# Gate-matrix stores issued from GpSimd, exponentials and first dots one step later

## The reference

```python
def peer(x, w_q, sub_keys, u, v):            # x: 512 x 1024
    qb = (xb @ w_q).reshape(TOKEN_BLOCK, 8, 2, 128)
    s = jnp.einsum('thcd,hcnd->thcn', qb, sub_keys)
    s_top, i_top = lax.top_k(s, 16)           # 16 of 128 keys, for each half
    cand = s_top[:, :, 0, :, None] + s_top[:, :, 1, None, :]
    best, pos = lax.top_k(cand, 16)           # 16 of 256 pairs; expert = i0*128 + i1
    g = jax.nn.softmax(best, axis=-1)
    h = jax.nn.gelu(jnp.einsum('td,thkd->thk', xb, u[eidx]))
    return jnp.einsum('thk,thkd->td', g * h, v[eidx])
```

## Time and profile before

| | |
|---|---|
| Device time, three runs | 1592.0, 1596.01, 1598.8 us; median 1596.01 |
| Profiled execution, own time | 1596.0 us |
| Its span | 1594.2 us |
| TensorE busy | 1572.1 us, 99% of the span |
| VectorE busy | 1319.1 us, 83% |
| ScalarE busy | 647.3 us, 41% |
| GpSimd busy | 486.9 us, 31% |
| Granted clock of TensorE, mean | 0.996 |
| DMA | 452.24 MB, 284 GB/s on the mean |

### The profile page before, as it was taken

One profiled execution on the slowest core, in us unless ns is written; L12 is line 12 of the kernel. 1 busy time (PEld: TensorE's weight loads), 2 busy tenths in 40 slices (PEclk: granted clock), 3 DMA queues, 4 the chain that ended last, 5 costly groups with the idle time before them and its releaser, 6 DMA issues.

```text
span 1594.2 us, 24556 instructions
## 1 busy us (share of the span) xinstructions
PE 1572.1 (99%) x9566; PEld 1394.9 (88%) x9566; DVE 1319.1 (83%) x2408; ACT 647.3 (41%) x1012; POOL 486.9 (31%) x243
## 2 busy tenths in 40 slices
PE   9999999999999999899999999999999999999998
PEld 8897977888989999899999999999988888888886
DVE  6564366345899999999998889999999999999997
ACT  5634355532223343345555334333333343343332
POOL 4433223352235038511010333333332332232200
PEclk9999999999999999999999999999999999999999
DMA  7872212145132998699998999999999999999971
GB/s 280 298 276 79 77 54 80 60 153 185 54 93 77 318 312 276 255 325 318 352 351 268 350 421 423 407 408 405 406 420 409 396 397 414 395 390 416 400 296 54
DMA packets 148547, 452.24 MB, mean 284 GB/s; under 512 B 12112, under 2 KB 73808, under 8 KB 127184
## 3 DMA queue, kind: packets, MB, share of 16 engines
q1 hardware_dynamic: 120528, 282.86, 49.0%
q0 software_dynamic: 23296, 151.04, 23.6%
q10 hardware_dynamic: 4608, 16.78, 2.6%
HBM read 395.55 MB, written 54.53 MB: 282 GB/s over the span
## 4 chain that ended last, share of the span: by engine, by line
PE 77%; DVE 18%; DMA 3%; issue 1%; ACT 1%; POOL 0%; SPq 0%; DVEq 0%; POOLq 0%; ACTq 0%
PE bank L1518 23%; PE bank L1520 23%; PE bank L1519 23%; PE bank L1824 3%; DMA h_scratch<-hout 2%; DVE idx L1259 1%; DVE idx L1251 1%; DVE val L1250 1%; DVE val L1258 1%; DVE tmp L1252 1%; DVE uvb L1363 1%; DVE wlo L1345 1%; PE bank L1660 1%; PE bank L1647 1%; PE bank L1617 1%
## 5 line engine op out<-in xcount | busy, mean ns | idle before, releaser
L1518 PE MATMUL bank<-xhi,whi 128*128 128x352 f32 (+1 forms) x1408 | 489.7, 348 | 9.8 <-DVE wlo L1345 5.9
L1520 PE MATMUL bank<-xhi,wlo 128*128 128x352 f32 (+1 forms) x1408 | 481.9, 342 | 0.0
L1519 PE MATMUL bank<-xlo,whi 128*128 128x352 f32 (+1 forms) x1408 | 481.7, 342 | 0.0
L760 POOL DMA_INDIRECT uvb<-in_uv,eidx x128 | 214.6, 1677 | 551.6 <-DVE acc L1391 405.7
L970 ACT ACTIVATE whi<-raw 128x1024 fp32r<-128x1024 f32 x220 | 231.8, 1056 | 179.5 <-PE bank L1520 156.2
L1518 PE MATMUL bank<-whi,ahi 128*128 128x512 f32 x762 | 296.6, 389 | 0.0
L1519 PE MATMUL bank<-wlo,ahi 128*128 128x512 f32 x762 | 296.5, 389 | 0.0
L1520 PE MATMUL bank<-whi,alo 128*128 128x512 f32 x762 | 296.5, 389 | 0.0
L1518 PEld LDWEIGHTS bank<-xhi,whi 128*128 128x128 f32 x1408 | 266.3, 189 | 26.8 <-DVE wlo L1345 6.2
L1519 PEld LDWEIGHTS bank<-xlo,whi 128*128 128x128 f32 x1408 | 266.8, 189 | 14.9
L1520 PEld LDWEIGHTS bank<-xhi,wlo 128*128 128x128 f32 x1408 | 266.1, 189 | 15.4
(11 more groups left out here) (229 smaller groups left out, 2007.3 us busy)
## 6 DMA issues: line engine op xcount, KB each, us to landing
raw<-in_u SPq DMA_DIRECT2D x118, 512.0 KB, 6.8
raw<-in_uv SPq DMA_DIRECT2D x102, 512.0 KB, 9.7
g_scratch<-stage SPq DMA_DIRECT2D x48, 512.0 KB, 6.8
gl<-g_scratch SPq DMA_DIRECT2D x32, 768.0 KB, 8.6
raw<-in_w_in SPq DMA_DIRECT2D x22, 1024.0 KB, 5.4
h_scratch<-hout SPq DMA_DIRECT2D x96, 192.0 KB, 6.1
hl<-h_scratch SPq DMA_DIRECT2D x24, 768.0 KB, 10.8
x<-in_uv SPq DMA_DIRECT2D x25, 512.0 KB
```

What stands on the lines that cost most here:

```text
L760: nc.gpsimd.indirect_dma_start(out=uvb[:, r % UVB, :], out_offset=None, in_=a["uv"][:, :], in_offset=bass.IndirectOffsetOnAxis(ap=eidx[:, ...
L1518: mm(out, lh, rh, start=first, stop=False)
L1519: mm(out, lh, rl, start=False, stop=False)
L1520: return mm(out, ll, rh, start=False, stop=last)
```

## The change

The store of the gate matrix moves from SyncE's program to GpSimd's. GpSimd's program behind the low parts becomes a loop over steps: gathers are issued in it ahead of the stores where their `gather_step` is not later, and all four stores of a set are issued together at step last + 1, after a wait for the set's last quad. Nothing else of SyncE's order changes. The exponentials go from ScalarE's step 36 to 37. The first six pairs of dots for the c rows go from steps 37, 38, 39, 40, 41, 43 to 38, 39, 40, 41, 42, 43.

```diff
-EXP_STEP = 36
+EXP_STEP = 37
-C_STEPS = [37, 38, 39, 40, 41, 43] + [46 + 3 * i for i in range(NCP - 6)]
+C_STEPS = [38, 39, 40, 41, 42, 43] + [46 + 3 * i for i in range(NCP - 6)]
+def sets_in(step):
+    for k in range(SETS):
+        last = next(t for t in range(NT) if QS * (k + 1) - 1 in quads_after(t))
+        if step == last + 1:
+            yield k
+def gather_step(r):
+    if r < UVB + NCP:
+        return C_STEPS[r - UVB] - 3
+    return SUM_STEPS[(r - UVB - NCP) // 2] - 2
...
-            def g_store(k, i):
-                sp.wait_ge(g_free, QS * (k + 1))
...
-                sp.dma_start(g_dram[quads, :, k, :, :].rearrange("q m n t -> m q n t"),
...
-                for k, i in set_of_step(s):
-                    g_store(k, i)
...
+            def g_store(k, i):
+                pool.wait_ge(g_free, QS * (k + 1))
...
+                nc.gpsimd.dma_start(g_dram[quads, :, k, :, :].rearrange("q m n t -> m q n t"),
...
-            for j in range(UVB, NCP):
-                gather_u(j)
-            pool.wait_ge(idx_done, 1)
-            for k in range(NG):
-                gather(k)
-                if k == UVB - 1:
-                    pool.wait_ge(cdot_gelu, 1)
...
+            r = UVB
+            for s in range(2 * NT):
+                while r < NCP + NG and gather_step(r) <= s:
+                    if r < NCP:
+                        gather_u(r)
+                    else:
+                        if r == NCP:
+                            pool.wait_ge(idx_done, 1)
+                        gather(r - NCP)
+                    if r - NCP == UVB - 1:
+                        pool.wait_ge(cdot_gelu, 1)
...
+                    r += 1
+                for k in sets_in(s):
+                    for i in range(4):
+                        g_store(k, i)
```

More of the change, by code:

```diff
@@ L622, in h_store @@
                 sp.dma_start(h_dram[n // 4][:, n % 4, :], hout[:, n % 4, :]).then_inc(h_stored[n % 4], 16)
-            def g_store(k, i):
-                sp.wait_ge(g_free, QS * (k + 1))
-                rows = slice(i * (NT // 4), (i + 1) * (NT // 4))
-                quads = slice(i * (NT // 16), (i + 1) * (NT // 16))
-                sp.dma_start(g_dram[quads, :, k, :, :].rearrange("q m n t -> m q n t"),
-                             stage[:, k % 2, rows, :].rearrange("m (q n) t -> m q n t", n=4)).then_inc(g_stored[k % 2], 16)
             def h_load(m):
@@ L644, in g_load @@
                 sp.dma_start(gl[:, i % 2, :, :, :], g_dram[v_tile(4 * i) // 4]).then_inc(g_in[i % 2], 16)
[L646 to L652, removed]
             sp.wait_ge(ln_out, TC)
@@ L762, in gather @@
                     in_offset=bass.IndirectOffsetOnAxis(ap=eidx[:, k:k + 1], axis=0)).then_inc(uv_in[r % UVB], 16)
+            def g_store(k, i):
+                pool.wait_ge(g_free, QS * (k + 1))
+                rows = slice(i * (NT // 4), (i + 1) * (NT // 4))
+                quads = slice(i * (NT // 16), (i + 1) * (NT // 16))
+                nc.gpsimd.dma_start(g_dram[quads, :, k, :, :].rearrange("q m n t -> m q n t"),
+                             stage[:, k % 2, rows, :].rearrange("m (q n) t -> m q n t", n=4)).then_inc(g_stored[k % 2], 16)
             for s in range(PRE_FIRST):
@@ L773, in _ @@
                     gather_u((s - 24) // 3)
-            for j in range(UVB, NCP):
-                gather_u(j)
-            pool.wait_ge(idx_done, 1)
-            for k in range(NG):
-                gather(k)
-                if k == UVB - 1:
-                    pool.wait_ge(cdot_gelu, 1)
-                    for g in range(CG):
-                        nc.gpsimd.dma_start(ch[CP:P, g * CT:(g + 1) * CT], cgel[g * CT:(g + 1) * CT, :]).then_inc(ch_in, 16)
+            r = UVB
[9 more added lines that the diff above has]
+                        pool.wait_ge(cdot_gelu, 1)
+                        for g in range(CG):
+                            nc.gpsimd.dma_start(ch[CP:P, g * CT:(g + 1) * CT], cgel[g * CT:(g + 1) * CT, :]).then_inc(ch_in, 16)
+                    r += 1
+                for k in sets_in(s):
+                    for i in range(4):
+                        g_store(k, i)
         @block.scalar
```

## The result

The changed kernel takes 1597.84 us (median of 20 runs, 1595.0 to 1604.1), the kernel before, run beside it, 1592.52 us (20 runs, 1589.5 to 1600.7). The ratio is 1.003 [1.002, 1.004]: 0.3% slower, some 5 us, where a gain of 4 us was forecast. It is inside the range given, and on the wrong side of the kernel before. The profiled execution took 1604.1 us, span 1602.3, against 1596.0 and 1594.2: 8.1 us more of span. They lie 6.2 and 3.5 us above the medians of their kernels, so the 8.1 us of the traces stand against 5.3 in the medians.

What follows compares the result with a forecast made beforehand. TensorE, busy 99% of the span, was taken as the bound, so only its idle or low-clock stretches could give time. 1596.0 - 4.8 (stores) + 0.8 (dots, clock) = 1592.0 us; range 1586 to 1606.

Steps and rivals of the forecast that it cites:

- Stores from GpSimd: 896 to 960 us: tile loads and `hout` stores no longer queue behind set 11; gain 4.8 us, ends 0 and 5.2.
- The waits of 918 and 924: TensorE's idle times of 2.27 us until 918.15 and 0.98 us until 924.75, on `hout`; forecast to go.
- the second rival: Last stretch, from 896 us: bound by the DMA engines anyway; gain about 1 us, 1595.8 us; chance 0.27.
- the third rival: Behind 896 us: set 11's stores hold up gathers 9 and 10, delaying dots; about 1598 us; chance 0.08.
- rival 1: Sets 2 to 11: long GpSimd store issue frees stage buffers late; 1606 us at 3.5 us per store; chance 0.15.
- First dots at steps 38 to 43: 652.5 to 692 us: tile 38 starts 2.3 us earlier, idle returns before one-hots; clock loss 0.8 us, ends 0 and 1.8.
- the third batch: One-hot matmuls at 691.5 us, forecast to start as before; starting well before or after would prove the prediction wrong.
- Exponentials at step 37: ScalarE near 652 us: exponentials at most some 1.3 us later, covered by over 4 us; cost 0.
- the other signs: Tile loads issued in about 0.4 us, ScalarE never waiting for `g_scratch` stores, next stop at 940 to 956 on `g_scratch` loads.
- 3 were named as a sign of being wrong: 896 to 960 us: TensorE still losing 3 us or more there would prove the prediction wrong.
- The issue on GpSimd: Each gate store takes 2.0 us to issue on GpSimd, 8 us for a set, covered by stage buffer reuse of 19.4 us.

Runs made afterwards that it cites:

- set 11 from SyncE: The changed kernel, but SyncE stores set 11 at its old steps 86 and 87; 1.0000 [0.9986, 1.0013] of the kernel before.
- 1.22 MB taken out: The changed kernel with set 11 not stored, its place filled with a second copy of set 9's data; 0.9985 [0.9969, 1.0002] of the kernel before.
- steps alone: The kernel before with exponentials at step 37 and first dots at 38 to 43, stores still from SyncE; 1.0005 [0.9985, 1.0025] of the kernel before.
- after again: Second execution and trace of the changed kernel, nothing altered; 1.0044 [1.0028, 1.006] of the kernel before.
- stores alone: The changed kernel with exponentials and dots at their old steps, gate stores from GpSimd; 1.0037 [1.0018, 1.0056] of the kernel before.
- set 11 ahead and old steps: The changed kernel with set 11's stores before gathers 7 and 8, exponentials and dots at old steps; 0.9994 [0.9979, 1.001] of the kernel before.
- set 11 ahead: The changed kernel with set 11's four stores before gathers 7 and 8 in GpSimd's order; 1.0007 [0.9986, 1.0028] of the kernel before.
- set 11 further behind: The changed kernel with set 11's stores behind gathers 9 and 10; 1.0026 [1.0013, 1.004] of the kernel before.
- the last one: The changed kernel with set 11's stores before gathers 7 and 8 and two pairs of dots later; 0.9998, then 0.9994 of the kernel before.

## Why the prediction was wrong, step by step

**The step that failed** is "Stores from GpSimd", in its last part: "In the last stretch tile loads and `hout` stores no longer stand in line behind 2 MB of set 11 ... 4.8 us." The waits of 918 and 924 did go, as said. Two things stand in their place.
- The gain has size 0 here. With set 11 from GpSimd in time, with set 11 from SyncE, and in before, the stretch takes 74.5 to 76.4 us and the runs agree within the intervals, at a DMA share of 1.01 to 1.03 and 408 to 415 GB/s in all of them. With 1.22 MB taken out it is 2.2 us shorter (one trace), with another issuer it isn't: it is bound by the DMA engines, and TensorE's idle time shows where the queue was noticed, not what it cost. That is the second rival, which had 0.27 and was read from the earlier trace rows. The Trainium skill (DMA: Bandwidth & Descriptors, Issuing engines are not separate DMA queues) says that a second issuer saves issue time only; the measurements of this stretch agree, and go further: the 6.05 us of issue were not worth anything either.
- The move has a price of some 5 us, which the third rival had in part (0.08, "about 1598"): set 11's stores behind gathers 7 and 8. The prediction saw that they start late ("about 900.5", measured 901.67) and asked only whether they land by step 94 and whether dots come late. The price is in the engines' work: over tiles 85 to 101, 1.09 MB more fell into the stretch than in before (2.7 us at 410 GB/s), since less of set 11 was moved ahead of it (before had issued its first two stores at 893.8), and the share was 1.00 in place of 1.03 over 81 us (2.4 us). Together that is 5.1 of 5.4 us. Part of the lower share is the gap of 900 to 906 (0.6 to 0.8 MB, 1.4 to 2.0 us); another is a second dip near the end (970 to 974 at 328 GB/s in after), behind TensorE's stops. This split is worked out from single traces and not tested term by term. That the place of set 11's stores in the queue is the cause is shown by the two pairs of kernels that differ in it alone.

Rivals 2 and 3 were treated as cases that exclude each other. The runs read better as one mechanism: an issue that comes late costs time because the engines are full from then on. No kernel had the late issue without the full engines, so this is a reading.

**Inside the range by luck.** The range reached up to 1606 for the sake of rival 1, the long issue, which is false, and the sum started from 1596.0, a profiled execution 3.5 us above the median of 20 runs, 1592.52. From that median the same terms give 1588.5, and 1597.84 is 9.3 us above it.

**First dots at steps 38 to 43**: the mechanism is right, the price of the clock was put too low. Tile 38 waits 3.67 us (said: 3.6) and starts at 654.09 (653.8); the new idle time before the first one-hots is 3.38 us at 683.32 (2 at 683); another 1.45 follows. The clock then falls to its lower level, as was weighed:
```profile
686.00:688.00 2.00, 2.00 (x18) 2.00 (x17) 2.00 (x4) 0.85 (x2) 0.00 (x0) 0.50 1.02 416
```
The granted clock is 0.75 in the 2 us before and 0.50 to 0.54 until 692. The net cost to tile 50 is 1.5 us (0.8 said, 0 to 1.8 given; 1.4 in the kernel with the steps alone), but it is a difference of two terms. From tile 43 to 50 after takes 5.0 us longer than before, 2.4 of it more idle time at the one-hots and 2.6 us beside it, which the lower clock of 684 to 692 is left to explain; the forecast had 1.8 at most. What made up for it was not forecast: behind its shorter stop tile 38 took 5.7 us in place of 6.9. So the third batch started at 693.39 and not at 691.5, which the prediction had named as a sign of being wrong. A loss of clock at 954 to 960, not foreseen, came with the new stop there: the chain's matmuls there are 0.29 us apart, where they are 0.16 at full clock.

**Exponentials at step 37**: cost 0, as said; no wait for the weights appears in the list of waits. Of the other signs, tile loads were issued in 0.33 us (0.4 said); ScalarE did wait for gate stores, three times, 4.3 us in all, and TensorE didn't notice (204.00 us busy of 204.00). TensorE's next stops came at 944 and 955, where they were expected, but on stores of `hout` and not on loads of `g_scratch`, and it stood idle for 9.0 us between 896 and 960, where 3 were named as a sign of being wrong.

**The issue on GpSimd**: 2.0 us were taken for a store of 1024 runs, with 0.51 and 5.8 as the ends. It is (min/median/max, ns):
```profile
L766 POOL DMA_DIRECT2D g_scratch<-stage x48: 887/897/984, 706.1 to 904.4; - x48
```
The first rival (0.15) is false, and (0.90 - 0.51)/992 makes 0.4 ns for a run, where 1.5 were taken. The reading that the prediction took from the Trainium skill (DMA: Bandwidth & Descriptors, Anatomy of one DMA), nearer 1 us, came out right; the page itself has no figure, and its "small, variable" agrees with 0.90 us for 1024 runs.

**What stays open.** After tile 101 the kernels with GpSimd's stores and late set 11 take 623.0, 623.0 and 623.9 us to the end (after, after again, stores alone), and the one with set 11 ahead and old steps 623.0, where the others take 621.8 to 622.7; it wasn't located. Why the `hout` wait near tile 96 is 9.6, 9.5 and 9.6 us in after, after again and stores alone and at most 4.8 with set 11 further behind was not settled either. Nor was it tested what the stores' move is worth by itself when two pairs of dots come later.

## What to carry to other kernels

Where a stretch's DMA share is at 1, price a change by bytes and by when they are issued, not by the waits that it removes: the waits move, the bytes stay. The same issue stall that was worth nothing there seems to have cost 2 us elsewhere, where VectorE had no lead left. A transfer that is moved to another queue must be put at the place in that queue's order where its data come ready; four stores behind a gather that waits 7 us cost 5 to 6 us here, and moving them ahead cost nothing that could be measured. Look at a stretch in small windows for a dip of the DMA share as well as for the stall, which here came 20 to 50 us later.

## What the runs showed of the hardware beyond that

- *A direct store from GpSimd makes few, large packets.* 48 stores of 1024 runs of 512 bytes added 6,912 packets, 144 each; from SyncE's queue they were 1,040 each. The bandwidth of the full stretch was the same, some 410 GB/s (408 and 412 in before; 411 and 413 with all sets from GpSimd and set 11 ahead).
- *VectorE's small operations beside GpSimd.* The selection ends either near 647 or near 652.5 us, in kernels whose code up to there is the same (the one with set 11 from SyncE, 646.9; after, 652.6). VectorE, then GpSimd, in the trace of before:
```profile
603.77 4.79 DVE L1321 TENSOR_TENSOR jf<-bposf,sel 128x128 bf16<-128x128 bf16 x1
```
```profile
603.63 4.77 POOL L738 TENSOR_TENSOR wlo<-raw,whi 128x1024 fp32r<-128x1024 f32 x2
```
An operation of 128x128 elements lasts as long as the two of GpSimd that it meets. Where it meets none it is short:
```profile
572.48 0.29 DVE L1321 TENSOR_TENSOR jf<-bposf,sel 128x128 bf16<-128x128 bf16 x1
```
The difference between 647 and 652.5 lies in such operations: in all fourteen traces VectorE's last 100 instructions of the selection start between 587.1 and 588.3, its idle time in the last 400 is 3.5 us, and its operations of 128x128 elements that last over 1 us there add up to 43.5 to 46.0 us in the traces with the late end and to 37.0 to 39.7 in those with the early one. Which of them meet seems to be settled by small shifts. That one kernel can come out either way is inferred: one set of timed runs of before lies in two groups (25 of 35 in 1585 to 1594.3 us, 10 in 1595.6 to 1599), the other sets less clearly; in the eight traces with the late end that have timed runs beside them the profiled execution lies 2.9 to 7.0 us above their median, in the five with the early end 2.6 us below to 0.3 above. Against it, the three kernels that were traced twice (before, after, the last one) showed the same end both times.
- *The clock after a short stop is not settled by the stop's length.* TensorE's first matmul of tile 38 in the kernel with the steps alone, then in the one with set 11 ahead:
```profile
654.55 0.66 PE L1518 MATMUL bank<-xhi,whi 128*128 128x352 f32 x1 [3.08 <-DVE wlo L1345]
```
```profile
654.80 0.43 PE L1534 MATMUL bank<-xhi,whi 128*128 128x352 f32 x1 [3.08 <-DVE wlo L1361]
```
After 3.08 us of idle time each, the granted clock over 655 to 660 is 0.70 in the first and 1.00 in the second, and the tile's gelu follows its first matmul by 5.7 and by 4.2 us: 1.5 us, which is the size that the loss had at 918 in the earlier trace rows too.
